# A two-block transformer on one core: high and low activations as one 512-column moving operand, and low parts of z weights on VectorE

## The reference, cut to what matters

```
u    = rms_norm(x, norm1_g)
proj = u @ w_in                      # q, k, v (3 x 1024) and z (3 x 1024 + 288)
attn = dilated_attention(q, k, v)    # 16 heads
rw   = rwkv7_time_mix(z, ...)        # the recurrent branch, 16 heads
x    = x + concat(attn, rw) @ w_out
u    = rms_norm(x, norm2_g)
gate, up = split(u @ w_gate_up)      # 2 x 5632
x    = rms_norm(x + (silu(gate) * up) @ w_down, final_g)

proj = rms_norm(x, norm1_g_2) @ w_in_2 + b_in_2     # conv and attention inputs
x    = x + concat(conv_group(...), swa_group(...)) @ w_out_2
xn   = rms_norm(x, norm2_g_2)
q    = xn @ peer_w_q                 # 2048 x 2048, then top-16 of 16384 experts for 8 heads
y    = sum over chosen experts of gate * gelu(xn . u_e) * v_e
out  = x + y
```

## Time and profile before

| | us |
|---|---|
| median of 3 runs | 3611.99 (3610.41 to 3619.82) |
| profiled execution, whole | 3615.79 |
| its span in the trace | 3614.0 |
| PE busy | 3363.7 (93%) |
| POOL busy | 2487.9 (69%) |
| DVE busy | 1516.1 (42%) |
| ACT busy | 1475.4 (41%) |
| HBM read | 548.33 MB |

### The profile page before, as it was taken

How to read it: one execution, slowest core, us unless ns; L and a number is a source line. 1 busy time by engine, 2 the same in 40 slices (tenths; PEclk the granted TensorE clock), 3 DMA queues, 4 the chain that set the end, 5 groups by cost and what they waited for, 6 DMA issues and landing times.

```text
span 3614.0 us, 74928 instructions
## 1 busy us (share of the span) xinstructions
PE 3363.7 (93%) x29214; PEld 3287.2 (91%) x29214; DVE 1516.1 (42%) x2503; ACT 1475.4 (41%) x1957; POOL 2487.9 (69%) x1063
## 2 busy tenths in 40 slices
PE   7789977989999999888778999999999999999999
PEld 6788867989999999887678999999999999999999
DVE  2058555432222200169921295667650366016600
ACT  4344522444444333444434454334344334433433
POOL 5654600768888788654346787777788778877787
PEclk9999978999999999988889999999999999999999
DMA  5843400546555556533234555555556555655555
GB/s 172 187 134 116 130 12 25 168 141 181 184 181 181 170 180 189 165 117 94 93 97 143 157 181 179 163 169 156 173 169 182 174 173 162 187 175 173 163 180 169
DMA packets 158089, 555.35 MB, mean 154 GB/s; under 512 B 17249, under 2 KB 23585, under 8 KB 157841
## 3 DMA queue, kind: packets, MB, share of 16 engines
q1 hardware_dynamic: 151008, 540.08, 48.8%
q0 software_dynamic: 2192, 8.20, 1.3%
q10 hardware_dynamic: 4768, 5.36, 0.5%
HBM read 548.33 MB, written 5.24 MB: 153 GB/s over the span
## 4 chain that ended last, share of the span: by engine, by line
PE 83%; DVE 11%; issue 3%; POOL 1%; ACT 1%; DMA 1%; POOLq 0%; ACTq 0%; DVEq 0%; SPq 0%
PE ps L528 74%; DVE ps L1638 2%; PE ps L715 2%; PE ps L584 1%; PE ps L902 1%; POOL wl L474 1%; DVE misc L1333 1%; PE ps L545 1%; DMA raw<-w_qkv 1%; DVE arena L1607 1%; DVE misc L1605 0%; DVE under_ul L1298 0%; DVE el L1773 0%; DVE arena L1608 0%; DVE arena L1435 0%
## 5 line engine op out<-in xcount | busy, mean ns | idle before, releaser
L474 POOL TENSOR_TENSOR wl<-raw,wh 128x1024 fp32r<-128x1024 f32 (+1 forms) x1034 | 2473.3, 2398 | 1028.3 <-ACT wh L976 1027.8
L976 ACT ACTIVATE wh<-raw 128x1024 fp32r<-128x1024 f32 (+1 forms) x1034 | 1085.3, 1052 | 1715.8 <-PE ps L528 1652.0
L528 PE MATMUL ps<-uh,wh 128*128 128x256 f32 x5584 | 1610.2, 288 | 84.3 <-DVE ul L1311 43.9
L528 PE MATMUL ps<-ul,wh 128*128 128x256 f32 x5584 | 1595.6, 286 | 0.0
L528 PE MATMUL ps<-uh,wl 128*128 128x256 f32 x5584 | 1595.0, 286 | 0.0
L528 PEld LDWEIGHTS ps<-uh,wh 128*128 128x128 f32 x5584 | 1089.3, 195 | 97.6 <-DVE ul L1311 45.5
L528 PEld LDWEIGHTS ps<-ul,wh 128*128 128x128 f32 x5584 | 1089.0, 195 | 0.5
L528 PEld LDWEIGHTS ps<-uh,wl 128*128 128x128 f32 x5584 | 1088.5, 195 | 0.0
L528 PE MATMUL ps<-el,wh 128*128 128x256 f32 x2048 | 574.0, 280 | 0.0
L528 PE MATMUL ps<-eh,wh 128*128 128x256 f32 x1536 | 439.7, 286 | 9.2 <-DVE el L1773 5.6
L528 PE MATMUL ps<-eh,wl 128*128 128x256 f32 x1536 | 430.3, 280 | 0.0
(11 more groups left out here) (312 smaller groups left out, 2983.4 us busy)
## 6 DMA issues: line engine op xcount, KB each, us to landing
raw<-w_u SPq DMA_DIRECT2D x256, 512.0 KB, 3.6
raw<-w_v SPq DMA_DIRECT2D x256, 512.0 KB, 3.6
raw<-w_gu SPq DMA_DIRECT2D x176, 512.0 KB, 3.6
raw<-w_down SPq DMA_DIRECT2D x80, 512.0 KB, 3.7
raw<-w_out SPq DMA_DIRECT2D x64, 512.0 KB, 3.6
raw<-w_z SPq DMA_DIRECT2D x54, 512.0 KB, 3.7
raw<-w_in SPq DMA_DIRECT2D x52, 512.0 KB, 3.6
raw<-w_qkv SPq DMA_DIRECT2D x48, 512.0 KB, 4.3
```

The source lines that it names most:

```text
L474: pool.tensor_tensor(wl[:, slot, 0:width], raw[:, slot, 0:width], wh[:, slot, 0:width].bitcast(F32), ALU.subtract).then_inc(lo_ready, 1)
L528: ins = pe.matmul(out, w[:, slot, at], x(c), start=first and c == n == 0, stop=last and c == kt - 1 and n == 2)
L976: act.activation(wh[:, slot, 0:width], raw[:, slot, 0:width], ACT.Copy).then_inc(hi_ready, 1)
```

## The change

Three parts.

1. `uh` and `ul` become the halves of one tensor `uhl`, `gh` and `gl` of `ghl`; `eh` and `el` lie in one tensor `ehl` of three parts. `pair_unit` multiplies `wh` with high and low activations in one instruction of 512 columns, into a whole PSUM bank (high product in columns 0:256, low product in 256:512), and `wl` with the high ones into columns 0:256. It is used in ten stages: qkv (its first 32 units), gu, down, out2, wq, u2, u3, v0, v1, v2. The stages z, out, in2, u0, u1, v3 and the v part of qkv keep three products of 256 columns.
2. The two halves of a bank have to be added. DVE does that: `add_halves` (a reduction of 512 to 256 columns) for qkv and wq in place of ACT's copy; for gu (into `GS` and into banks 4 and 5) and for u2 and u3 (into banks 4 to 7) ahead of ACT's silu and gelu; and a second residual add after down, out2, v0, v1 and v2 tiles.
3. In the z stage POOL makes the low parts of the first four units only; DVE makes the other 50, two behind `divide` of each step. ACT takes over the squares of the scaled keys (`kk_sq`), and its exponentials for a pair move one step later.

```
+            def pair_unit(b, ready, slot, pair, k0, kt=UKT, first=True, last=True):
+                pe.wait_ge(lo_ready, ready)
+                for c in range(kt):
+                    at = slice(c * P, (c + 1) * P)
+                    pe.matmul(bank(b).rearrange("p (n t) -> p n t", n=2), wh[:, slot, at], pair[:, :, k0 + c, :],
+                              start=first and c == 0, stop=False, skip_group_check=True)
+                    ins = pe.matmul(bank(b)[:, 0:T], wl[:, slot, at], pair[:, 0, k0 + c, :], start=False,
+                                    stop=last and c == kt - 1, skip_group_check=True)
+                return ins
...
-            for c in range(27):
-                if c < NH:
-                    bias(c)
-                for j in range(2):
-                    g = BASE["z"] + 2 * c + j
-                    split(g + 1, g % RING)
+            splits(BASE["z"], RING)
+            for h in range(NH):
+                bias(h)
+            pool.wait_ge(lo_ready, BASE["out"])
...
-                    act.wait_ge(w_used, i * 4 + (2 * j + 2))
-                    act.activation(QK[:, bass.ds(i * 2 + j, 1), :], ps[:, j:j + 1, 0:T], ACT.Copy)\
-                        .then_inc(qkv_ev, 1)
...
+                    act.wait_ge(z_ready, 3 * i + 5)
+                    act.activation(sc[:, 3, :], RK[:, i % 2, 1, :], ACT.Square, scale=prm("kk", i)).then_inc(kk_sq, 1)
...
-                    act.activation(GS[:, j, :], bank(2 * j)[:, 0:T], ACT.Silu).then_inc(gs_ready, 1)
+                    act.wait_ge(gate_sum, i * 2 + (j + 1))
+                    act.activation(GS[:, j, :], GS[:, j, :], ACT.Silu).then_inc(gs_ready, 1)
...
+            def add_halves(out, b):
+                return dve.tensor_reduce(out, bank(b).rearrange("p (n t) -> p t n", n=2), AX, ALU.add)
...
+            take_sums(QK, "qkv", qkv_ev)
...
-                link(dve.tensor_scalar(kk, k, prm("kk", i), None, ALU.mult))
-                dve.tensor_tensor(sq, kk, kk, ALU.mult).then_inc(kk_sq, 1)
...
+                for g in range(BASE["z"] + 2 * c + RING, BASE["z"] + 2 * c + RING + 2) if c < 25 else ():
+                    if g == BASE["z"] + RING:
+                        dve.wait_ge(lo_ready, g)
+                    dve.wait_ge(hi_ready, g + 1)
+                    dve.tensor_tensor(wl[:, g % RING, :], raw[:, g % RING, :], wh[:, g % RING, :].bitcast(F32),
+                                      ALU.subtract).then_inc(lo_ready, 1)
...
+                    product = bank(4 + j)[:, 0:T]
+                    dve.wait_ge(w_used, i * 8 + (BASE["gu"] + 4 * j + 2))
+                    add_halves(GS[:, j, :], 2 * j).then_inc(gate_sum, 1)
                     dve.wait_ge(w_used, i * 8 + (BASE["gu"] + 4 * j + 4))
+                    add_halves(product, 2 * j + 1).then_inc(up_sum, 1)
...
-                    dve.tensor_tensor(gl[:, at, :], GS[:, j:j + 1, :], gh[:, at, :].bitcast(F32), ALU.subtract)\
+                    dve.tensor_tensor(gl[:, at, :], ps[:, 4 + j:5 + j, 0:T], gh[:, at, :].bitcast(F32), ALU.subtract)\
...
+                    dve.tensor_tensor(x, x, ps[:, j:j + 1, T:2 * T], ALU.add).then_inc(res_low, 1)
+                    dve.wait_ge(res_low, i * 2 + (j + 1))
+                    dve.tensor_tensor(x, x, ps[:, j:j + 1, 0:T], ALU.add).then_inc(res_ready, 1)
...
+            def sum_experts(q, i, lows_of=None):
+                for j in range(4):
+                    dve.wait_ge(w_used, i * 8 + (BASE[f"u{q}"] + 2 * j + 2))
+                    dve.wait_ge(u_ev, i * 4 + (QJ * q + j - 3))
+                    add_halves(bank(4 + j)[:, 0:T], j % 2).then_inc(exp_sum, 1)
+                    if lows_of is not None:
+                        expert_low(lows_of, 2 * j)
+                        expert_low(lows_of, 2 * j + 1)
```

More of the change, by code:

```diff
@@ L530, in unit, with pair_tile @@
                 return ins
+            def pair_unit(b, ready, slot, pair, k0, kt=UKT, first=True, last=True):
[7 more added lines that the diff above has]
+                return ins
+            def pair_tile(b, g, pair, second=None):
+                for n in range(2):
+                    if n and second:
+                        pe.wait_ge(*second)
+                    pair_unit(b, g + (n + 1), (g + n) % RING, pair, UKT * n, first=n == 0, last=n == 1)\
+                        .then_inc(w_used, 1)
             def tile(out, g, slot, xh, xl, second=None):
@@ L555, in loop @@
                         pe.wait_ge(evac, i * 4 + (before + at + j - 1))
-                        tile(bank((at + j) % 2)[:, 0:T], i * 8 + (g0 + 2 * j), (g0 + 2 * j) % RING, uhc, ulc)
+                        for n in range(2):
+                            g = g0 + 2 * j + n
+                            pair_unit((at + j) % 2, i * 8 + (g + 1), g % RING, UHL, UKT * n, first=n == 0, last=n == 1)\
+                                .then_inc(w_used, 1)
             uhc = lambda c: uh[:, c, :]
@@ L794, in gate_up @@
                     if not first:
-                        pe.wait_ge(gp_ready, i * 2 + (j // 2 - 1))
-                    tile(bank(j)[:, 0:T], i * 8 + (g0 + 2 * j), (g0 + 2 * j) % RING, uhc, ulc,
-                         (u_ready, 2 * DT) if first and j == 0 else None)
+                        pe.wait_ge(up_sum, i * 2 + (j // 2 - 1))
+                    for n in range(2):
+                        g = g0 + 2 * j + n
+                        if first and j == 0 and n:
+                            pe.wait_ge(u_ready, 2 * DT)
+                        pair_unit(j, i * 8 + (g + 1), g % RING, UHL, UKT * n, first=n == 0, last=n == 1)\
+                            .then_inc(w_used, 1)
             gate_up(0, True)
@@ L877, in _ @@
                     pe.wait_ge(res_ready, 2 * DT + c - 1)
-                tile(bank(c % 2)[:, 0:T], g, g % RING, lambda c: uh[:, (c + WT) % DT, :],
-                     lambda c: ul[:, (c + WT) % DT, :], None if c else (ml_ready, 2 + WT + 4))
+                for n in range(2):
+                    if c == 0 and n:
+                        pe.wait_ge(ml_ready, 2 + WT + 4)
+                    pair_unit(c % 2, g + (n + 1), (g + n) % RING, UHL, WT * (1 - n), first=n == 0, last=n == 1)\
+                        .then_inc(w_used, 1)
             norm_sum(4, mix2)
@@ L952, in _ @@
                 pe.wait_ge(res_ready, (2 + q) * DT)
-                with pe.Fori(0, 8) as i:
+                experts_in(q, 0, first=True)
+                with pe.Fori(1, 8) as i:
                     experts_in(q, i)
@@ L1326, in _, with take_sums @@
             scale(0, "n1", 0)
+            def take_sums(out, name, done):
+                with dve.Fori(0, DT // 2) as i:
+                    for j in range(2):
+                        dve.wait_ge(w_used, i * 4 + (BASE[name] + 2 * j + 2))
+                        add_halves(out[:, bass.ds(i * 2 + j, 1), :].rearrange("p a t -> p (a t)"), j)\
+                            .then_inc(done, 1)
+            take_sums(QK, "qkv", qkv_ev)
             def row_max(h, logits, ready):
@@ L1782, in _ @@
                 gate(0, 7, m, True)
-            expert_lows(0)
+            for k in range(8):
+                expert_low(0, k)
             def add_out(q, i, last):
```

128 lines of the change are left out of this document (76 added, 52 removed).

## The result

The changed kernel took **3553.8 us** (median of four runs, 3537.3 to 3558.2) against 3611.2 us for the kernel before (four runs, 3606.8 to 3619.8): ratio 0.983, interval 0.981 to 0.985. It is faster by 57 us, where 85 were forecast; the time lies inside the range of 3460 to 3565 us. The profiled execution is the slowest of the four, 3558.2 us, with a span of 3556.3 us against 3614.0 before.

The account below looks back on a forecast made before the run. PE was taken as the bound, busy 93% of the span, with its large products 74% of the chain of waits. The terms, -72 - 23 + 4 + 6 = -85 us, took 3612 to 3527 us; range 3460 to 3565.

Parts of the forecast that it names:

- term 1: Ten stages with wide products: one load and start less in each of 5440 weight blocks, -72 us.
- A block then costs 225 + p instead of 3p: Weight block with one 225 ns wide product and one narrow product of p ns, saving 2p - 225: 10.6 to 15.0 ns.
- Term 2: z stage: DVE's 128x2 instruction no longer stalls beside POOL's subtractions, -23 us, ends 0 and -32.
- Term 3: Adding the two halves of a bank on DVE, hidden inside stages, waited for at stage ends: +4 us, 0 to +10.
- Term 4: u2 and u3: DVE's low parts of experts, slowed beside POOL, delay the sums PE waits for: +6 us, 0 to 14.
- the wait that I worked out from 7.1: u2 and u3: DVE needs 7.1 us per tile against PE's 5.5, so PE waits some 1.5 us twice.
- at no cost: POOL's feed of low parts: a PE unit shrinks to 2.76 us, POOL needs 2.40, leaving 0.36 us cover per unit.
- A: Rival: the load hides behind 512 columns, so a wide product costs its columns alone; 3463 us, chance 0.25.
- B: Rival: in z, DVE's subtractions delay the next head's maxima as much as the stall did; 3550 us, chance 0.12.
- C: Rival: the 512 columns come in two pieces, a wide product takes 315 ns; slower, 4017 us, chance 0.05.
- D: Rival: products are halved in number but the wide one's pitch is 240 ns; 3599 us, chance 0.03.
- The forecast case: Whole kernel: the terms as forecast, wide products at 225 ns, 3527 us, 2.4% faster, chance 0.55.

Follow-up runs that it names:

- the changed kernel again: The changed kernel, unaltered, run once more with a second profile: 3537.9 us, ratio 0.981 to the kernel before.
- the grouped order: The changed kernel with each unit's eight 512-column products first, then its eight 256-column ones: 3534.4 us, ratio 0.979; once more, 3534.5 us.

## Why the prediction was right in sign and short of its size

The time lies inside the range, and that is in part luck. The upper end, 3565 us, was drawn for a z stage that gains nothing. The z stage gained more than forecast, and the room was used up by term 1. In the profiled executions the ten stages gave 32.6 us less than forecast, z 6.6 more, v3 lost 4.3 and the rest gained 3.0: 27 us short in all.

*Term 1 was mis-sized: -72 forecast. Taken stage by stage against the kernel with narrow products in their place, it was -27 in the profiled run and in the one with z's low parts on POOL, and -38 to -42 in the three others.* The step that failed is "A block then costs 225 + p instead of 3p". It took 225 ns from the norm sum and p from one profile of before, as if both were fixed. The runs show that what stands on top of the columns is a pace of the whole row. Added up, columns alone make 2560 ns of a unit; before, 320 or 267 ns stood on top for 24 starts, after it 267, 233 or 213 for 16. The fast pace (346.7) is close to my 345, and saves the 13.3 ns of one start against 360. At the slow one (353.3) it saves half of that. In down the forecast went from 355.8 ns a block to 343.6; the profiled run had 353.3 before and 353.3 after, other runs 349. The part that fell short most, and in every profile, is v0 to v2: 16.3 us forecast, 3.0 measured against narrow products. There two units went from 6080 ns to 6008 and 6052 in turn, 3 ns a block where I had 10.6. Had every stage had its faster pace throughout, 3200 blocks would have saved 13.3 ns and 2240 about 4.5: 53 us, which is the most that this term holds with long and short products in turn.

A part of the rest is the clock. v1 starts at half speed in all profiles with wide products in the changed kernel's order, and at full speed in the kernel before, after 1.8 us in which PE is idle in both. Windows of the first 4 us of v1, the kernel before and then the changed kernel again:

```profile
2840.70:2844.70 4.00, 4.00 (x34) 4.00 (x35) 4.00 (x5) 0.92 (x1) 1.72 (x1) 1.00 0.65 189
```

```profile
2766.00:2770.00 4.00, 3.98 (x13) 3.40 (x14) 4.00 (x6) 0.00 (x0) 1.76 (x1) 0.57 0.61 175
```

The granted clock is 0.57 instead of 1.00, and the first unit takes 4450 ns instead of 2925, which eats v1's gain of 1.5 us whole. The kernel with narrow products in the wide ones' place, with all its sums, starts v1 at full clock again (2925 ns), so it goes with the wide products and not with DVE's work. With the grouped order v1 starts at full clock too (2885 to 2889 ns). I had no term for this, and why the alternating order lowers the clock was not tested.

*Term 2 was right in mechanism and too careful: -23 forecast, -29.6 measured.* The stall of 3.3 us was the cause, and L1389 takes the 0.17 us expected. Steps 0 to 4 take 40.5 us (forecast 42) and 5 to 16 110.1 (115), against 39.9 and 108.4 of PE's own work. The 9 us of excess that I left for DVE's order were 2.3. The squares that I folded in as a small relief are worth, with the exponentials that moved along, 3.7 us of the second part, more than the 3 us of DVE's time.

*Term 3: +4 forecast, -1 to -3 measured* (with the wide product given as two). The sum of two halves takes 698 ns as estimated (0.69), and the hidden layer's low part out of PSUM 425 ns instead of 2.30 us; gu's end got 1.4 us shorter, as against the 1.1 of the text. The ends of v0, v1 and v2 cost 0.2 us each or less, not 0.42; down took 0.7 more.

*Term 4: +6 forecast, about +1 measured.* Eight subtractions of u3 in the kernel after:

```profile
L1841 DVE TENSOR_TENSOR ehl<-hb,ehl 128x1024 fp32r<-128x1024 f32 x8 | 17.6, 2234 | 5.9 <-ACT ehl L1298 5.9
```

They take 2.23 us each on average, not the 3.2 of the earlier trace rows. One of the four pairs fell into a pause of POOL and took 2.48 us for both; the others took 4.7 to 5.7. A tile's work on DVE is then 0.70 + 4.47 = 5.2 us, below PE's 5.5, and the wait that I worked out from 7.1 does not build up. The small wait that did come is another one. Meanwhile POOL's subtractions take 3.39 us each instead of 2.40, without a pause between, and a unit of PE takes 2.77. So the feed falls behind, until PE waits for `wl`; POOL and PE in u3:

```profile
L482 POOL TENSOR_TENSOR wl<-raw,wh 128x1024 fp32r<-128x1024 f32 x4 | 13.4, 3388 | 0.0
```

```profile
3016.19 0.51 PE L543 MATMUL ps<-uhl,wh 128*128 128x512 f32 x1 [0.24 <-POOL wl L482]
```

That is the sign of being wrong that I had named (POOL's idle time near 0, with PE waiting for `wl`), for some 13 us of the stage. Three units of u3 are longer by 0.12, 0.51 and 0.10 us and two of u2 by 0.15 and 0.10, 1.0 us in all. With narrow products, whose units take 2.88 us, no unit is longer. I had put the feed "at no cost", with a cover of 0.36 us a unit; beside DVE's subtractions there is no cover. So the size was overestimated and the mechanism was wrong: what PE waits for is the feed, not the sums.

*Not in the sum:* v3 lost 4.3 us in the profiled run and 0.7 in the next two, by its pace alone.

*The rivals.* A (load hidden, 0.25) is out: 225 to 241 ns for a wide product in every row at full clock. B (DVE in POOL's place, 0.12) is out: PE is busy all through steps 0 to 16. C (two pieces) is out, since nothing comes near its 315 ns, and in down one piece is no faster. D (pitch 240, 0.03) was nearer than its chance: at the slow pace the wide starts are 236 ns from the next on average. The forecast case had 0.55, and what came was a case between it and D that had no place among the rivals: that the pitch is not one number.

## What to carry to other kernels

A pitch that is read from one long row of products is a state of that run, so read it in several stages and runs of unchanged code first, and give a term that saves a few ns in each of thousands of products the width of that spread. Where one engine's short instruction ended to the tick with another engine's work, nearly the whole stall was gained when that work went, up to the bottleneck engine's own work in that stretch. If long and short products share a unit, try them in groups: here six stages had one pace in three profiles, and it was the fastest version. A change that shortens the bottleneck's unit also takes away the cover of the engine that feeds it: set the feeder's time beside it in the stage where it is slowest.

## What the runs showed of the hardware that I had not expected

- Rows of products have exact, discrete paces: 2880 or 2827 ns (once 2840) for 24 products of 256 columns, 2827, 2793, 2791 or 2773 for 8 of 512 and 8 of 256. A pace can hold for hundreds of microseconds, and differs between runs of one program: gu at 850 or 867 blocks in 300 us. What picks it was not found; a single extra product can switch it, and eight small products every 6 us make two paces take turns (6008 and 6052 ns).
- After the same 1.8 us without work, v1 starts at a granted clock of 1.00 in the five kernels with narrow or grouped products before it (first unit 2885 to 2925 ns), and at 0.57 to 0.61 for its first 4 us in all six profiles with wide and narrow ones in turn (4446 to 4462 ns).
- At half clock none of this stands on top: a block of 768 columns takes 640 ns, 768 / 1.2 exactly, before and after.
- A DVE instruction on 128x2 elements takes 4.98 us beside two POOL subtractions and 0.17 without them; a 128x1024 subtraction with both inputs in SBUF takes 1.22 us alone, 3.27 in a row beside POOL and 2.23 in spaced pairs beside it, where POOL's own take 3.39 instead of 2.40. One with an input in PSUM (128x256) takes 0.43 beside the same POOL work, where it took 2.30 out of SBUF.
